# Attention over pairs of heads: one matrix scaled by GpSimd and the other by VectorE, scores in two equal pieces, the last value product over 128 rows padded with zeros

## What is computed

```
# A: 4 heads of two query/key halves, width 64; values of width 128
s = q @ k^T * scale + bias                 # 528 keys
p = softmax(s);  attn = p[0] - lam * p[1]; out = attn @ v
# B: 8 heads of width 64, 2 key/value heads
out = softmax(q @ k^T * scale) @ v         # 528 keys
# C: 16 heads of width 64, 2 key/value heads, window of 128, sink
keys = 16 meta + band of up to 384;  s = q @ k^T * scale + bias, masked
out = softmax(concat(s, sink))[..., :-1] @ v
```

## Time and profile before

| | before |
|---|---|
| median of three runs | 2428.13 us |
| profiled execution, its own time | 2426.36 us |
| its span (first to last instruction) | 2424.6 us |
| TensorE matmul (PE) busy | 2248.2 us, 93% |
| TensorE weight load (PEld) busy | 1866.2 us, 77% |
| VectorE (DVE) busy | 1149.3 us, 47% |
| ScalarE (ACT) busy | 786.1 us, 32% |
| GpSimd (POOL) busy | 940.6 us, 39% |
| both scalings of GpSimd, L754 and L755 | 52 operations each |

### The profile page before, as it was taken

How to read it: one execution, slowest core, us unless ns; L and a number is a source line. 1 busy time by engine, 2 the same in 40 slices (tenths; PEclk the granted TensorE clock), 3 DMA queues, 4 the chain that set the end, 5 groups by cost and what they waited for, 6 DMA issues and landing times.

```text
span 2424.6 us, 33777 instructions
## 1 busy us (share of the span) xinstructions
PE 2248.2 (93%) x13234; PEld 1866.2 (77%) x13234; DVE 1149.3 (47%) x1672; ACT 786.1 (32%) x1271; POOL 940.6 (39%) x436
## 2 busy tenths in 40 slices
PE   3696968999999998899999998999999999999996
PEld 2695645999999975688888877778866788887875
DVE  4656753552053314465025344857564455443224
ACT  2122645332122326532222322324422332322223
POOL 0331037344444436544444433324332444444442
PEclk9797989999999999999999999999988999999998
DMA  5752000233333350033333346323322333332331
GB/s 141 137 189 62 1 1 1 80 95 87 95 87 95 88 183 1 18 90 93 96 96 95 93 120 135 111 66 85 83 78 61 94 97 95 95 95 85 92 89 57
DMA packets 371761, 209.92 MB, mean 87 GB/s; under 512 B 25936, under 2 KB 362929, under 8 KB 370753
## 3 DMA queue, kind: packets, MB, share of 16 engines
q1 hardware_dynamic: 353088, 184.21, 26.4%
q10 hardware_dynamic: 18560, 24.13, 4.4%
HBM read 196.85 MB, written 15.41 MB: 88 GB/s over the span
## 4 chain that ended last, share of the span: by engine, by line
issue 39%; PE 32%; POOL 19%; DVE 5%; ACTq 2%; ACT 1%; DMA 1%; POOLq 0%; SPq 0%; DVEq 0%
POOL w_lo L731 17%; PE acc L800 8%; PE acc L801 8%; PE acc L802 8%; PE ops L902 3%; PE acc L875 2%; ACTq L1349 2%; PE tps L891 1%; DVE probs L1921 1%; POOL probs L754 1%; POOL probs L755 1%; PE ops L889 1%; DVE root L2251 1%; PE tps L859 0%; DVE rstd L1865 0%
## 5 line engine op out<-in xcount | busy, mean ns | idle before, releaser
L731 POOL TENSOR_TENSOR w_lo<-raw,w_hi 128x1024 fp32r<-128x1024 f32 x328 | 805.0, 2454 | 1262.2 <-ACT w_hi L1253 1247.2
L1253 ACT ACTIVATE w_hi<-raw 128x1024 fp32r<-128x1024 f32 x327 | 346.6, 1060 | 1140.4 <-PE acc L802 1077.4
L800 PE MATMUL acc<-hr_hi,w_hi 128*128 128x512 f32 x1120 | 451.2, 403 | 8.7 <-POOL w_lo L731 4.9
L801 PE MATMUL acc<-hr_lo,w_hi 128*128 128x512 f32 x1120 | 446.1, 398 | 0.0
L802 PE MATMUL acc<-hr_hi,w_lo 128*128 128x512 f32 x1120 | 445.6, 398 | 0.0
L800 PE MATMUL acc<-hn_hi,w_hi 128*128 128x264 f32 (+1 forms) x896 | 266.5, 297 | 38.7 <-POOL w_lo L731 34.6
L801 PE MATMUL acc<-hn_lo,w_hi 128*128 128x264 f32 (+1 forms) x896 | 263.9, 294 | 0.0
L802 PE MATMUL acc<-hn_hi,w_lo 128*128 128x264 f32 (+1 forms) x896 | 263.5, 294 | 0.0
L800 PEld LDWEIGHTS acc<-hr_hi,w_hi 128*128 128x128 f32 x1120 | 212.5, 190 | 66.1 <-issue 10.8
L802 PEld LDWEIGHTS acc<-hr_hi,w_lo 128*128 128x128 f32 x1120 | 212.5, 190 | 51.5
L801 PEld LDWEIGHTS acc<-hr_lo,w_hi 128*128 128x128 f32 x1120 | 212.5, 190 | 50.5 <-issue 0.7
(11 more groups left out here) (364 smaller groups left out, 3811.5 us busy)
## 6 DMA issues: line engine op xcount, KB each, us to landing
raw<-in_w_up SPq DMA_DIRECT2D x64, 512.0 KB, 4.0
raw<-in_w_down SPq DMA_DIRECT2D x64, 512.0 KB, 3.8
raw<-in_w_in SPq DMA_DIRECT2D x56, 512.0 KB, 3.8
raw<-in_w_ffn_gate SPq DMA_DIRECT2D x22, 512.0 KB, 3.8
raw<-in_w_ffn_up SPq DMA_DIRECT2D x22, 512.0 KB, 3.8
raw<-in_w_in_even SPq DMA_DIRECT2D x18, 512.0 KB, 7.5
raw<-in_w_ffn_down SPq DMA_DIRECT2D x16, 512.0 KB, 3.7
bias_c<-bias_c_d SPq DMA_DIRECT2D x1, 5392.0 KB, 17.6
```

What stands on the lines that cost most here:

```text
L731: nc.gpsimd.tensor_tensor(w_lo[:, part], raw[:, slot], w_hi[:, part].bitcast(F32), ALU.subtract).then_inc(sems["lo"], T.up("lo"))
L800: mm(out, w_hi[:, part, w0 + k, :], xh, start=s0, stop=False)
L801: mm(out, w_hi[:, part, w0 + k, :], xl, start=False, stop=False)
L1253: fn(w_hi[:, n % 2], raw[:, n % 4], ACT.Copy).then_inc(sems["hi"], T.up("hi"))
```

## The change

GpSimd scales the first matrix of a pair and signals a new semaphore `scaled`; VectorE scales the second one in `shares`, behind its own reciprocals, and signals `probs`; `turn` waits for both. This is for B and C. In A and B the scores are made in two pieces of 264 columns (HALF) instead of 16 and 512, for which the accumulator is read from another column; in B the keys then stand in their own order, meta keys last, in A the stored keys are rotated, which `even_tile` does with two operations for each of four tiles. `metaT_1` and the meta part of the values get 128 rows; they are cleared once per use by VectorE, which signals `cleared`, and ScalarE waits for that ahead of its copies and, in C, of the swap of keys. The last product then runs over 128 rows, 112 of them zeros.

```diff
-            metaT_1 = sb(s, "metaT_1", [N_META, 2, 2, P])
+            metaT_1 = sb(s, "metaT_1", [P, 2, 2, P])
...
-            p.keys = [(0, N_META, keys(SEQ, N_META)), (N_META, SEQ, keys(0, SEQ))]
-            p.tiles = [N_META + P * k for k in range(4)]
+            p.keys = [(c, HALF, keys(c, HALF)) for c in (0, HALF)]
+            p.meta = meta
+            p.tiles = [(0 if meta else N_META) + P * k for k in range(4)]
...
-                p.v = [[vtok_e[:, k, vc:vc + 64] for k in range(4)] + [vtok_e[0:N_META, 4, vc:vc + 64]]] * 2
+                p.v = [[vtok_e[:, k, vc:vc + 64] for k in range(4)] + [vtok_e[:, 4, vc:vc + 64]]] * 2
...
-                    S = [probs_1[0:p.nq, s % RING, o, 0:p.width] for o in range(2)]
-                    nc.gpsimd.tensor_scalar(S[0], S[0], st[:, 4:5], None, ALU.mult)
-                    nc.gpsimd.tensor_scalar(S[1], S[1], st[:, 5:6], None, ALU.mult).then_inc(
-                        sems["probs"], T.up("probs"))
+                    S = probs_1[0:p.nq, s % RING, 0, 0:p.width]
+                    nc.gpsimd.tensor_scalar(S, S, st[:, 4:5], None, ALU.mult).then_inc(
+                        sems["scaled"], T.up("scaled"))
...
-                            bank = flat[o][:, S_AT:] if p.wide else acc[s % 2][:, o, :]
+                            bank = flat[o][:, LEAD:] if p.wide else acc[s % 2][:, o, :]
...
                     pe.wait_ge(sems["probs"], probs_0 + s + 1)
+                    if not p.differ:
+                        pe.wait_ge(sems["scaled"], scaled_0 + s + 1)
...
-                        nc.tensor.transpose(meta, S[:, 0:N_META], unit)
+                        nc.tensor.transpose(meta, S[:, p.meta:p.meta + N_META], unit)
...
-                    fn(metaT_1[:, s % 2, first:, 0:p.nq], meta, ACT.Copy).then_inc(sems["metas"], T.up("metas"))
+                    fn(metaT_1[0:N_META, s % 2, first:, 0:p.nq], meta, ACT.Copy).then_inc(sems["metas"], T.up("metas"))
...
             project(even_in, norm_heads, first=parameters)
             all_stored()
+            T.saw("cleared", 2)
+            act.wait_ge(sems["cleared"], T.at("cleared"))
             tokens_first(vtok_e, (0, P, 2 * P, 3 * P, 4 * P))
...
             act.wait_ge(sems["sink_key"], T.at("sink_key"))
+            T.saw("cleared", 2)
+            act.wait_ge(sems["cleared"], T.at("cleared"))
             swap_keys(k_o[:, 1, :], k_o[:, 0, :])
...
                     if not p.differ:
                         v.reciprocal(st[:, 4:6], st[:, 2:4]).then_inc(sems["recip"], T.up("recip"))
+                        dve.wait_ge(sems["recip"], T.at("recip"))
+                        S = probs_1[0:p.nq, s % RING, 1, 0:p.width]
+                        v.tensor_scalar(S, S, st[:, 5:6], None, ALU.mult).then_inc(sems["probs"], T.up("probs"))
                         return
...
+                elif x < 8:
+                    dve.wait_ge(sems[f"full{b}"], T.at(f"full{b}"))
+                    v.tensor_tensor(qkv_e[:, x, 0:N_META], acc1[b][:, SEQ:LEN], rstd[:, SEQ:LEN], ALU.mult).then_inc(
+                        sems["dve"], T.up("dve"))
+                    store(v.tensor_tensor(qkv_e[:, x, N_META:LEN], real(acc1[b]), real(rstd), ALU.mult), b)
...
                     dve.wait_ge(sems["ssm_out"], T.at("ssm_out"))
+                    v.memset(vtok_e[:, 4, :], 0.0).then_inc(sems["cleared"], T.up("cleared"))
...
             dve.wait_ge(sems["stored1"], T.at("stored1"))
+            v.memset(metaT_1[:], 0.0).then_inc(sems["cleared"], T.up("cleared"))
             T.saw("rope_in", 16)
...
             v.memset(k_o[:, 0, LEN:LEN + 16], 0.0).then_inc(sems["sink_key"], T.up("sink_key"))
+            v.memset(vtok_o[:, 4, :], 0.0).then_inc(sems["cleared"], T.up("cleared"))
...
             dve.wait_ge(sems["bias_in"], T.at("bias_in"))
+            v.memset(metaT_1[:], 0.0).then_inc(sems["cleared"], T.up("cleared"))
             for at in (N_META, BAND_W + N_META):
```

More of the change, by code:

```diff
@@ L35 @@
 LEAD = 512 - HALF
-S_AT = 512 - N_META
 DT = D_MODEL // P
@@ L450, in transposed_blocks_program @@
             "gate", "gated", "mixed_hi", "mixed_lo",
-            "negmax", "exp", "recip", "eps_rows", "probs", "p_full", "p_stored", "metas",
+            "negmax", "exp", "recip", "eps_rows", "scaled", "probs", "p_full", "p_stored", "metas",
             "dve", "act",
@@ L454, in transposed_blocks_program @@
             "bias_rows", "bias_out", "bias_a_out", "bias_c_out", "bias_in", "lam", "lam_sum",
-            "sink_key", "rope_in", "swap_ready", "rot_in", "roped", "kswap_in",
+            "sink_key", "cleared", "rope_in", "swap_ready", "rot_in", "roped", "kswap_in",
             "mixer_ready", "h_scaled", "tab_in", "u_ready", "u_out", "u_in", "state_in", "toe_ready", "scanned",
@@ L509, in halves, with dense_pair @@
             return [(own if o == k else other)[64 * o:64 * o + 64, c:c + n] for o in range(2)]
-        def dense_pair(t, q, keys):
+        def dense_pair(t, q, keys, meta):
             p = Pair()
@@ L523, in transposed_blocks_program @@
                 p = dense_pair(t, qkv_e[:, hd, :], lambda c, n, hd=hd: [
-                    qkv_e[64 * o:64 * o + 64, 4 + hd, c:c + n] for o in range(2)])
+                    qkv_e[64 * o:64 * o + 64, 4 + hd, c:c + n] for o in range(2)], 0)
                 c0 = 384 - P * t if t < 4 else 400
@@ L528, in transposed_blocks_program @@
                 p.bias = [bias_a[0:p.nq, hd, c0:c0 + LEN]] * 2
-                p.v = [[vtok_e[:, k, hd * P:(hd + 1) * P] for k in range(4)] + [vtok_e[0:N_META, 4, hd * P:(hd + 1) * P]]]
+                p.v = [[vtok_e[:, k, hd * P:(hd + 1) * P] for k in range(4)] + [vtok_e[:, 4, hd * P:(hd + 1) * P]]]
                 p.dest = qkv_e[:, 8 + hd, q_cols(t)[0]:q_cols(t)[0] + p.nq]
@@ L556, in transposed_blocks_program @@
                 p.bias = [bias_c[:, 2 * i + o, b0:b0 + p.width] for o in range(2)]
-                p.tiles = [LEAD_2 + P * k for k in range(hi - lo)]
+                p.meta, p.tiles = 0, [LEAD_2 + P * k for k in range(hi - lo)]
                 vc = 64 * (i // 4)
-                p.v = [[vtok_o[:, k, vc:vc + 64] for k in range(lo, hi)] + [vtok_o[0:N_META, 4, vc:vc + 64]]] * 2
+                p.v = [[vtok_o[:, k, vc:vc + 64] for k in range(lo, hi)] + [vtok_o[:, 4, vc:vc + 64]]] * 2
                 p.dest = (mix_o_hi[:, i, c0:c0 + P], mix_o_lo[:, i, c0:c0 + P])
@@ L864, in attend @@
                 n = len(pairs)
-                stored_0, probs_0, copied_0 = (T.n.get(k, 0) for k in ("s_stored", "probs", "p_stored"))
+                stored_0, probs_0, scaled_0, copied_0 = (
+                    T.n.get(k, 0) for k in ("s_stored", "probs", "scaled", "p_stored"))
                 def scores(s):
@@ L913, in attend @@
                 T.saw("probs", n)
+                if not pairs[0].differ:
+                    T.saw("scaled", n)
                 T.saw("p_stored", n)
```

2 lines of the change are left out of this document (1 added, 1 removed).

## The result

The kernel before took 2428.6 us (median of 4 runs), the changed kernel **2389.23 us** (median of 4, 2386.82 to 2392.94): 0.9839 of before, 95% interval 0.9822 to 0.9856, some 39 us less. In two later sets of runs, on two chips, the same kernel came to 2392.44 us (0.986, 0.9833 to 0.9887) and 2395.2 us (0.9849, 0.9823 to 0.9875), 33 and 32 us less than the kernel before beside it.

A forecast was written before the change was run, and what follows sets the result against it. TensorE was taken to be held by GpSimd's second scaling, 26.0 us over B and C. Savings of 14 in B, 10.5 in C and 3.3 in A, less 0.5 for clearing, made 27.3: forecast 2400 us, range 2391 to 2411.

The forecast's parts named there:

- the sum: Whole kernel: B 14, C 10.5 and A 3.3 us saved, less 0.5 for clearing, 27.3 us in all.
- with a little for the clock: Last step of the forecast: from 2400.8 us against the median down to 2400 for TensorE's clock.
- rival 3: TensorE's clock may not fall after waits for GpSimd: up to 4 us less, 2391 with other bounds good; chance 0.09.
- 0.65 per step: B: each step falls from 4.30 to 3.65 us, over 20 pairs about 13 us.
- bind almost alike: B, tops to turn: GpSimd's path of 3.57 us and ScalarE's chain of 3.53 limit nearly equally after the split.
- 1.35 per four pairs: C: saving per four pairs from the split and padded product, by 8, less the ends, 10.5 us.
- 0.165 per step: A: half of TensorE's shorter work counts against ScalarE's chain, by 20, 3.3 us; bounds 0 and 6.6.
- about 1.15: A and B: the scores' eight matmuls in equal pieces should span this many us instead of 1.35.
- TensorE's saving of 0.33: A and B, per pair: 0.19 us from equal score pieces and 0.14 from the padded last product.
- Rival 1: B and C: GpSimd scales first and VectorE is held for its operation; about 2427 us, no change; chance 0.08.
- rival 2: B and C: VectorE is held and also scales at one element a cycle; about 2435 us, slower; chance 0.05.
- Rival 4: Shorter TensorE work brings nothing, only the split does: B 11, C 8, less the clearing, 2410 us; chance 0.12.

The follow-up runs named there:

- both_vector: The changed kernel with both matrices of a pair scaled by VectorE and none by GpSimd; median 2386.89 us, 0.9816 to 0.9857 of before.
- drain_filled: The kernel before with eleven unread identity products put into TensorE's waits behind B's last scores; median 2426.82 us, 0.9977 to 1.0009 of before.
- before_third: The kernel before, unchanged, profiled a third time; its three profiles are listed with medians of 2425 to 2430 us.
- before_again: The kernel before, unchanged, run and profiled once more; its three profiles are listed with medians of 2425 to 2430 us.

## Why the prediction was wrong by a little

The direction, the mechanism and the terms per step held. The step that failed is the last one of the sum: "with a little for the clock (rival 3)", 0.8 us where 4 to 6.5 belonged, and rival 3's "up to 4 us less".

- **B.** 0.65 per step was forecast, 0.685 measured (42.67 to 35.82 for ten). The turns are 3.56 apart instead of the 3.65 named. GpSimd was second and was held 0.32, not 0.43 (in wide C 0.24, where 0.42 was named and the times named for VectorE make 0.37); with that its path is 1.26 + 0.25 + 1.91 + 0.07 = 3.49 and ScalarE's copies are behind most of the waits that are left, as "bind almost alike" had it.
- **C.** 1.35 per four pairs was forecast, 1.37 measured; 8 x 1.37 = 11.0. The whole stage gave 10.0 in the mean: two of the changed kernel's groups of four took 11.87 and 12.01 us, and half clock at C's start differs between executions.
- **A.** 0.165 per step was forecast, 0.149 measured, 3.0 in all.
- **Scores and pad.** The scores' eight matmuls span 1.17 instead of 1.35 us, as "about 1.15" said. In steps the halves are worth 0.06 in A and 0.08 in B on top of the pad, twice that on TensorE if half counts, so 0.12 to 0.16 where the sum had 0.19; the pad alone comes to 0.14 to 0.18 where it had 0.14. The gap ahead of the last product is gone. That only half of TensorE's saving of 0.33 would count where its steps take turns with another wait held for A (0.149) and for B without the split (42.67 to 41.21 for ten, 0.146), against 0.165.
- **Clearing.** Forecast 0.5, measured 0.74 (0.23 us pass between VectorE's store and its clearing of 0.48).
- **VectorE's scaling.** 0.50, 0.43 and 0.36 us against 0.48, 0.42 and 0.36. Its queue had room to spare: a second scaling of 0.50 in it (both_vector) made the steps shorter, not longer.

Added up with the measured steps: 13.7 + 11.0 + 3.0 - 0.7 = 27.0, against 27.3 in the sum. **Most of what was missing is the clock.** In the first profile of before, half clock made the last two steps ahead of B's last tops 10.2 us where drain_filled has 8.6, the drain up to the first product 13.2 where before_third has 11.0, and the first tile 11.3 where drain_filled has 8.6: 1.6 + 2.2 + 2.7 = 6.5 us. In before_again the same three places cost 1.1 + 0.2 + 2.7 = 4.0, in before_third two steps cost 2.1. The changed kernel paid none of it in three profiles. So the mean is 4.2 us and the profiled execution had 6.5. The rows were there. The earlier trace rows show 0.76 granted over 12 us, which is 2.9 us of work lost, and the same view has the stretches in front of it and behind it, which the sum did not price:

```profile
333.00:412.00 79.00, 68.07 (x656) 43.79 (x654) 34.11 (x122) 45.12 (x107) 57.12 (x37) 0.94 0.01 1
424.00:429.00 5.00, 5.00 (x24) 5.00 (x25) 0.41 (x1) 0.00 (x0) 0.38 (x1) 0.54 0.35 105
```

0.54 over 5 us is another 2.3 us lost, and 0.94 over 79 us is 4.7, more than half of it at B's start. With 6.5 in place of 0.8 the forecast would have been 2394.

Other terms at nothing in the sum, from the experiments and the table of stages: the shorter half clock at B's start, at most 1.7 us; the way from A to B, 1.3 in the mean, where a stretch at half clock lasted 3.4, 13.6 and 10.3 us in the kernel before and 3.4 each time in the changed one; and the way behind B at full clock, where the drain falls from 11.0 to 9.4 us and the first tile from 8.6 to 8.2, 2.0 in all, of which the twentieth of the 20 steps holds 0.7. With C at its 10.0 this makes 27.0 + 4.2 + 1.7 + 1.3 + 1.3 - 1.0 = 34.5, against 33.7 for the mean of three profiles. The 39 us of the first result are some 5 more. In the first profiles 2.3 of them are clock in B and its drain and 3.3 are the stage behind C, whose code is the same and whose mean differs by 0.4. So that the result fell below 2391 is luck of its four runs; the later two sets came to 2392.44 and 2395.2, inside the range. That the clock was priced too low is not luck. The low end of the range had no room for it either: 2391 stood for every bound at its good end and the clock at "up to 4", and runs of the unchanged kernel spread over 10 us.

Rival 1 (2427) and rival 2 (2435) both rested on a hold of VectorE for GpSimd's whole operation. It isn't there in either order. The Trainium skill (SBUF — State Buffer, "Who interferes with whom") says that GpSimd and a VectorE operation in a two-port mode exclude each other for the whole instruction. This case's trace agrees for the low part of a weight unit, an operation of GpSimd with two inputs, and doesn't for the scaling by a column (GpSimd 0.17 to 0.30 us longer, VectorE 0 to 0.15). Why the two differ, no run here shows. Rival 4 (2410) fell: pad and halves without the split took 0.9937 of before.

## What to carry to other kernels

When an engine's wait is taken out of a stretch in which TensorE's clock falls now and then, price the fall by every half-clock stretch of the whole stage and its drain, and leave room for it in both directions, since unchanged code shows it at other places in other executions. Compare variants by the repeated step at full clock, which here agrees to 0.03 us in ten steps, and not by one time that carries 10 us of clock. Two engines that scale side by side cost each other little, but the faster of them alone does as well: on VectorE two operations of 0.50 us, one behind the other, took the place of one of 0.50 beside GpSimd's 1.90.

## What was not expected of the hardware

- GpSimd's scaling of 528 columns slowed from 1.60 to 1.90 us beside a scaling of VectorE that began 0.06 us earlier. With GpSimd first, VectorE slowed from 0.50 to 0.65 (0.43 to 0.47 for 401 columns, not at all for 273) and GpSimd not at all, whereas a VectorE copy of 16 columns beside GpSimd's two-input operation took 2.38.
- VectorE scaled 401 and 273 columns in 0.43 and 0.36 us. The odd widths cost nothing extra: from 528 to 401 and from 401 to 273 columns the mean falls by 0.064 and 0.067 us. The Trainium skill (Advanced Engine Details and Errata, "2x-2p Requirements") admits odd, equal widths to the fast mode; the trace agrees.
- Half clock came and went with unchanged code: from B's start to C 13.7, 10.2 and 6.8 us of it in three profiles of the kernel before, at other places each time. Idle time filled with products that nobody reads brought no time back. The half clock at B's start, though, was 20.5 us in ten profiles without the split and 17.1 in ten with it.
